# A decoder trunk with mixture of experts on one core: expert outputs weighted and added in place, the row list as one product, and reordered scores, taps and copies

## The reference, cut to what matters

```
y, _, v_rows = mixer(x)        # z = rms_norm(x) @ w_in -> u, v, a, b (512 channels each)
                               # v = layer_norm(gelu(v)); A = u * (masked 128x128 mix of v per chunk)
                               # B = silu(layer_norm(depthwise conv of a*sigmoid(b), width 31))
x = x + concat(A, B) @ w_out
x = x + attention(rms_norm(x) @ wq, K, V) @ wo     # prompt: K, V of 256 memory rows
                                                   # sample: 8 cached K, V sets, one for each token
g   = argmax(group logits)                         # 4 groups, 8 experts in each
w_e = softmax(top 2 logits of group g) * softmax(group logits)[g]
x = x + sum over the 2 experts of w_e * (silu(xt@w1) * (xt@w3)) @ w2      # inner width 256
y = rms_norm(x) * final_norm_g
```

## Time and profile before

| what | us |
|---|---|
| median of 3 runs | 679.25 (678.85 to 681.24) |
| the profiled execution's own time | 680.17 |
| its span in the trace | 678.4 |
| TensorE busy in it | 594.8 (88%) |
| VectorE busy | 317.4 (47%) |
| ScalarE busy | 197.9 (29%) |
| POOL busy | 79.8 (12%) |
| bytes moved | 181.57 MB, mean 268 GB/s |
| TensorE's mean granted clock | 0.944 |

### The profile page before, as it was taken

One profiled execution on the slowest core, in us unless ns is written; L12 is line 12 of the kernel. 1 busy time (PEld: TensorE's weight loads), 2 busy tenths in 40 slices (PEclk: granted clock), 3 DMA queues, 4 the chain that ended last, 5 costly groups with the idle time before them and its releaser, 6 DMA issues.

```text
span 678.4 us, 11951 instructions
## 1 busy us (share of the span) xinstructions
PE 594.8 (88%) x4899; PEld 466.9 (69%) x4899; DVE 317.4 (47%) x625; ACT 197.9 (29%) x337; POOL 79.8 (12%) x131
## 2 busy tenths in 40 slices
PE   5999999899999999999999957999999987589810
PEld 5999996577899999984889844546646654246400
DVE  4678787789644374778422273211111111011147
ACT  6422323145734344445022231111111111011032
POOL 0000000700002200000212201112112111010100
PEclk9999999999999999999989975999999999689965
DMA  8863110326554314779599495999999999999663
GB/s 325 306 243 124 63 64 3 127 84 212 164 167 149 125 64 137 271 243 424 208 391 393 160 399 199 402 421 418 420 417 420 421 418 421 420 421 414 250 271 127
DMA packets 35652, 181.57 MB, mean 268 GB/s; under 512 B 8943, under 2 KB 10127, under 8 KB 16765
## 3 DMA queue, kind: packets, MB, share of 16 engines
q1 hardware_dynamic: 26733, 165.62, 62.1%
q0 software_dynamic: 5600, 12.76, 5.0%
q10 hardware_dynamic: 3264, 2.42, 1.1%
HBM read 174.94 MB, written 15.61 MB: 281 GB/s over the span
## 4 chain that ended last, share of the span: by engine, by line
PE 65%; SPq 14%; DMA 8%; DVE 8%; issue 3%; ACT 1%; DVEq 0%; POOLq 0%; ACTq 0%
PE ps L1714 13%; PE ps L1716 13%; PE ps L1715 13%; SPq L628 9%; PE ps L2146 7%; SPq L637 4%; PE ps L2174 4%; DMA w<-exp_w 4%; PE ps L1821 4%; PE ps L1710 3%; DMA raw<-caches 2%; PE ps L1923 2%; DVE ttr_out L1354 1%; PE ps L1987 1%; DVE x L1662 1%
## 5 line engine op out<-in xcount | busy, mean ns | idle before, releaser
L1714 PE MATMUL ps<-xH,w_h 128*128 128x260 f32 x480 | 138.7, 289 | 0.4 <-DVE xL L1368 0.2
L1716 PE MATMUL ps<-xL,w_h 128*128 128x260 f32 x480 | 136.3, 284 | 0.0
L1715 PE MATMUL ps<-xH,w_l 128*128 128x260 f32 x480 | 136.1, 284 | 0.0
L2146 PE MATMUL ps<-w,xeT 128*64 128x256 f32 (+2 forms) x1024 | 121.5, 407 | 12.5 <-DMA w<-exp_w 10.3
L2146 PEld LDWEIGHTS ps<-w,xeT 128*64 128x64 f32 (+2 forms) x1024 | 82.9, 145 | 56.2 <-issue 29.5
L1714 PEld LDWEIGHTS ps<-xH,w_h 128*128 128x128 f32 x480 | 91.1, 190 | 5.0 <-issue 4.3
L1715 PEld LDWEIGHTS ps<-xH,w_l 128*128 128x128 f32 x480 | 91.1, 190 | 0.1
L1716 PEld LDWEIGHTS ps<-xL,w_h 128*128 128x128 f32 x480 | 91.1, 190 | 0.0
L1059 DVE TENSOR_TENSOR w_l<-raw,w_h 128x2048 fp32r<-128x2048 f32 x27 | 61.8, 2289 | 27.8 <-ACT w_h L741 27.6
L2174 PE MATMUL ps<-w,aT 128*64 128x512 f32 (+2 forms) x256 | 60.3, 628 | 15.8 <-DVE aT L1627 12.0
L741 ACT ACTIVATE w_h<-raw 128x2048 fp32r<-128x2048 f32 x27 | 51.6, 1911 | 22.2 <-PE ps L1716 19.3
(11 more groups left out here) (352 smaller groups left out, 857.0 us busy)
## 6 DMA issues: line engine op xcount, KB each, us to landing
w<-exp_w SPq DMA_DIRECT2D x96, 1024.0 KB, 24.0
raw<-weights SPq DMA_DIRECT2D x27, 1024.0 KB, 5.3
raw<-caches SPq DMA_DIRECT2D x16, 1024.0 KB, 7.4
qb<-q_rows POOLq DMA_DIRECT2D x4, 1024.0 KB, 6.7
yr<-y_rows SPq DMA_DIRECT2D x4, 1024.0 KB, 7.9
xT<-x_turned SPq DMA_DIRECT2D x4, 520.0 KB, 7.4
raw<-x_prompt SPq DMA_DIRECT2D x4, 512.0 KB, 12.0
x_rows<-x ACTq DMA_DIRECT2D x4, 512.0 KB
```

The lines of the kernel that those rows point to most:

```text
L1714: pe.matmul(out, h1, h2, start=start, stop=False)
L1715: pe.matmul(out, l1, h2, start=False, stop=False)
L1716: return pe.matmul(out, h1, l2, start=False, stop=stop)
L2146: last = pe.matmul((mm[0][half, j, 0:FF], ta[1][half, 0:FF])[h], xeT[j][:, k, half], w13[s][:, h, k, :], start=k == 0, stop=k == KT_D - 1)
```

## The change

Parts, in the order of the program:

1. V_TAPS is 11: VectorE does eight more part taps, TensorE 640 small products where it did 704.
2. VectorE does the v rows' scale and shift itself: two instructions for each piece and head, the first (x − mean) · gain, the second times the root plus bias. POOL does none of it.
3. VectorE's and ScalarE's order around the last sample scores is new. ScalarE: values_out(0), norms(3), split_h(25). VectorE: below.
4. The samples' outputs are turned by eight plain 128x128 transposes in two halves ("so0", "so1"), and copied from every 16th column.
5. The weights' five instructions stand ahead of count_p. A factor 0.5 doubles the weights, for part 7.
6. The list is one accumulation of ten products with `row_hot` as the stationary side and 32 moving columns; norm factor and weight are listed by ten more with 64 (`hot_two`). No parts.
7. VectorE adds the experts' output, times its slot's weight, onto the gathered rows (`rows_out`). Since both rows of a token now hold x + 2·w·y, their sum is twice the result; the final norm takes 4·EPS for that. The residual isn't read back, and the tail has one addition.
8. There are four row buffers `xe` in place of two and two `ye`. A gather into one waits for the scatter out of it. The third and fourth are cleared by POOL after the first two gathers.
9. The loop turns its first round's rows at its start; before, the last static round did that.
10. `kept_busy` adds products of ones with ones, whose result nobody reads: 14 at the start, 4 and 2 around the count, 20 ahead of the list, 12 and 4 around the first turn.
11. Some semaphores are merged, and ScalarE's table for Sqrt is loaded right after the loop.

```diff
-V_TAPS = 9
+V_TAPS = 11
+ROWS = 4
...
-            PART_AT = {4: 3, 5: 4, 6: 4, 7: 3, 8: 2, 9: 3, 10: 3, 11: 3, 14: 3}
+            PART_AT = {4: 3, 5: 4, 6: 4, 7: 3, 8: 2, 9: 3, 10: 3, 11: 3, 12: 2, 13: 2, 14: 3, 15: 2}
...
-                    last = dve.tensor_scalar(row, row, mv[0:n_t, j, h, 0:1], mv[0:n_t, j, h, 1:2], ALU.subtract, ALU.mult)
+                    last = dve.scalar_tensor_tensor(row, row, mv[0:n_t, j, h, 0:1], ln_g[0:n_t, c], ALU.subtract, ALU.mult)
                 last.then_inc(v_norm, 1)
+                dve.wait_ge(v_norm, j + 1)
+                for h in range(HEADS):
+                    row, n_t, c = v_row(j, h)
+                    last = dve.scalar_tensor_tensor(row, row, mv[0:n_t, j, h, 1:2], ln_b[0:n_t, c], ALU.mult, ALU.add)
+                last.then_inc(v_ready, 1)
...
-            sample_scores(5)
+            sample_scores(5, range(2))
             score_sums(3)
+            sample_scores(5, range(2, 4))
+            values_low(0)
+            sample_scores(6, range(2))
+            values_low(1)
             split_l(25)
-            values_low(0)
-            values_low(1)
-            sample_scores(6)
             values_low(2)
+            sample_scores(6, range(2, 4))
             values_low(3)
             sample_scores(7)
...
             dve.tensor_tensor(w_ex[:, 0, :], e_max[:, 1, :], e_max[:, 0, :], ALU.subtract).then_inc(g_dif, 1)
+            dve.wait_ge(g_exp, 1)
+            dve.tensor_reduce(g_sum[:], g_ex[:], AX_X, ALU.add)
+            dve.wait_ge(g_exp, 2)
+            link(dve.tensor_scalar(w_ex[:, 1, :], w_ex[:, 0, :], 1.0, 0.5, ALU.add, ALU.mult))
+            link(dve.tensor_tensor(w_ex[:, 1, :], w_ex[:, 1, :], g_sum[:], ALU.mult))
+            link(dve.reciprocal(wgt[:, 0, :], w_ex[:, 1, :]))
+            link(dve.tensor_tensor(wgt[:, 1, :], wgt[:, 0, :], w_ex[:, 0, :], ALU.mult))
...
+            dve.tensor_tensor(hot_two[:, :, :, 0, :], hot_col[:], rs_b, ALU.mult).then_inc(rs_hot_ready, 1)
+            dve.tensor_tensor(hot_two[:, :, :, 1, :].rearrange("p i t c -> p (i t) c"), hot_col[:].rearrange(flat),
+                              columns_of(wgt[:]), ALU.mult).then_inc(rs_hot_ready, 1)
...
-            def y_right(q, j, scattered):
+            def rows_out(q, i, weight):
...
-                dve.tensor_copy(ye[j][:, 512:D], mm[1][:, 1, :]).then_inc(yv_ready, 1)
+                for b in range(2):
+                    half = xe[i][:, 512 * b:512 * b + 512]
+                    dve.scalar_tensor_tensor(half, mm[1][:, b, :], weight, half, ALU.mult, ALU.add).then_inc(y_ready, 1)
...
-                link(dve.scalar_tensor_tensor(x2[0:n, t, :], yr[t][0:n, 0, :], wgt[0:n, 0, t:t + 1], x2[0:n, t, :],
-                                              ALU.mult, ALU.add))
-                dve.scalar_tensor_tensor(x2[0:n, t, :], yr[t][0:n, 1, :], wgt[0:n, 1, t:t + 1], x2[0:n, t, :],
-                                         ALU.mult, ALU.add).then_inc(y_sum, 1)
+                dve.tensor_tensor(x2[0:n, t, :], yr[t][0:n, 0, :], yr[t][0:n, 1, :], ALU.add).then_inc(y_sum, 1)
...
+            def kept_busy(out, count):
+
+                for _ in range(count):
+                    pe.matmul(out, ones[:], ones[:], start=True, stop=True)
+
+            pe.wait_ge(dve_made, 1)
+            kept_busy(ta[0][:, 0:P], 14)
             first_pair()
...
-            for k in range(8):
-                last = pe.matmul(out[:, k, :], o_s[:, k * P:(k + 1) * P], one_row, start=True, stop=True)
-            last.then_inc(tv_ready, 1)
+            for b in range(2):
+                pe.wait_ge(tv_used, TV_AT[f"or{b}"] + 1)
+                out = open_tv(f"so{b}")
+                for k in range(4):
+                    last = turn(out[:, k * P:(k + 1) * P], o_s[:, (4 * b + k) * P:(4 * b + k + 1) * P])
+                last.then_inc(tv_ready, 1)
...
+            pe.wait_ge(ta_used, len(TA_ORDER))
+            kept_busy(ta[1][:, 0:P], 20)
+            listed("ids", lambda n, i, j: hot_no[0:n, i, j, :])
+            pe.wait_ge(rs_hot_ready, 2)
+            listed("rs_ids", lambda n, i, j: hot_two[0:n, i, j].rearrange("p w c -> p (w c)"))
...
+            kept_busy(ta[1][:, 0:P], 12)
             pe.wait_ge(tv_used, len(TV_ORDER))
-            pe.wait_ge(ta_used, len(TA_ORDER))
-            gathered_columns(0, 0, 1)
+            gathered_columns(0, 1)
+            kept_busy(ta[1][:, 0:P], 4)
             for q in range(PAIRS):
                 hidden(q, q % 2, slots_of(q), q >= 2)
-                gathered_columns(q + 1, (q + 1) % 2, (q + 1) // 2 + 1)
+                if q + 1 < PAIRS:
+                    gathered_columns((q + 1) % ROWS, (q + 1) // ROWS + 1)
...
             for q in range(PAIRS):
                 pool.wait_ge(xt_done, q + 1)
-                gather(q % 2, gids[:, q + 2:q + 3])
-                pool.wait_ge(ya_ready, q + 1)
-                pool.wait_ge(yv_ready, q + 1)
-                scatter(q, q % 2, ids[:, q:q + 1])
+                i = (q + 2) % ROWS
+                if q + 2 >= ROWS:
+                    pool.wait_ge(y_stored[i], 16 * scattered(i, q + 2))
+                gather(i, gids[:, q + 2:q + 3])
+                pool.wait_ge(y_ready, 2 * (q + 1))
+                scatter(q % ROWS, ids[:, q:q + 1])
```

276 lines of the change are left out of this document (120 added, 156 removed).

## The result

The changed kernel takes 675.85 us in the median of 10 runs (673.57 to 677.55), the kernel before 679.37 (10 runs, 678.14 to 681.24): a ratio of 0.9947, with a 95% interval of 0.9932 to 0.9962. It is faster by 3.5 us where 7.95 was forecast. The profiled execution took 676.56 with a span of 674.8, so the two spans differ by 3.6.

The account below looks back on a forecast made before the run. TensorE was taken to hold most of the chain, then the expert-weight stream, restarted by round 0's gate. Terms sum to −7.95 from the profiled 680.17, giving 672.2; the median, 0.92 lower, was forecast at 671.4 us, range 665.5 to 678.

Parts of the forecast that it names:

- step (b): Routing: twenty products of ones ahead of the list take 6.0 us, ending just behind the one-hot rows it needs.
- step (d): Routing: twelve ones and second list end before the gather lands; turn takes 1.15 for 1.94, gate starts 418.7 for 417.55.
- Rival B's half-way case: Routing: the clock rises only in the list, so routing costs about +5 and the total is 676.5; chance 0.10.
- step (a): Routing: weight instructions ahead of count_p wait for the second exponential, putting count_p at 398.4, +2.0 us for the chain.
- Values: Values and sample scores: values_low(1) stands behind scores awaiting query rows, making TensorE late by +2.0 us, between 0 and 3.7.
- Sample rows: Turning the samples' outputs: eight transposes in halves start the output projection 1.4 earlier, clock staying up saves 1.6; −3.0 us.
- Rival C: Behind the sample rows: transposes leave the clock low, 1.6 us is lost, total 673.0; chance 0.08.
- Taps: Convolution: 64 of 704 products go, −2.4 us; v rows on VectorE cost nothing, with 3 us left at the take.
- Start: Program start: fourteen ones let the first pair run at full clock; −0.25 us, between 0 and −0.75.
- Loop entry: First loop round: its turn and copy move into the loop, 2.5 us at full clock, partly absorbed by weight waits; +1.1.
- Rival D: Rounds: gathers wait for scatters, which needs landings over 19 us; chance 0.07 together with Rival E.
- Rival E: Convolution stage: the v rows are late on VectorE by 11 us, total 682; chance 0.07 together with Rival D.

Follow-up runs that it names:

- e2: The changed kernel with VectorE's and ScalarE's order around the sample scores as before; 673.06 us, ratio 0.9905.
- e4: The changed kernel with V_TAPS back to 9, so 704 convolution products as before; 680.26 us, ratio 1.0003.
- e5: The changed kernel with the samples' outputs turned by products of 8 columns again, in the same two halves; 676.19 us, ratio 0.9946.
- e6: The changed kernel with the v rows' scale and shift on POOL again; 676.33 us, ratio 0.9961.
- e3: The changed kernel with the five weight instructions moved from ahead of count_p to behind row_hot; 671.65 us, ratio 0.9900.
- e11: The kernel before, unchanged, profiled a second time; 678.87 us in one execution.
- e1: The changed kernel without the 42 products of ones in routing, the 14 at the start kept; 676.74 us, ratio 0.9955.
- e12: e8 without the 14 products of ones at the start; 671.83 us, ratio 0.9892.
- e13: The kernel before with only 14 products of ones added ahead of the first pair; 677.27 us, ratio 0.9970.
- e10: The kernel before with the first of each tile's two additions in the tail left out, residual still read back; 673.38 us, ratio 0.9913.
- e7: The changed kernel with the changes of e2 and e3 together, all ones kept; 669.35 us, ratio 0.9850.
- e8: e7 without the twelve products of ones ahead of the first turn; 669.29 us, ratio 0.9843.
- e14: e8 with 7 products of ones at the start in place of 14; 669.26 us, ratio 0.9851.
- e9: e3 without the 42 products of ones in routing; 674.88 us, ratio 0.9936.

## Why the prediction was wrong

**Routing, step (b) and step (d): the steps that failed.** The prediction had "eight slow, twelve fast, 6.0 us" for the twenty ones, and the twelve ones ending before the gather. The first took 7.4, 14 or so at the lower level, for the clock rose only near 406, 6 us after they began and not 3.5. (In e2, e4, e5 and e6 it rose 2.8 to 5.4 us after they began and they took 5.9 to 7.1, so this part of the miss is between nothing and 1.4.) The lists took 2.6 and 2.9 us where 2.1 was taken. The twelve were half as fast as counted, because the clock falls under the second list or just as it ends (in all ten traces with ones ahead of the lists), and they held the turn for 2 us. 1.4 + 0.5 + 2.0 = 3.9 us is the miss of 3.95. The prediction had named a sign of being wrong, that ones are the bound in front of the list: they were, by 1.9 us. The estimate from one row at 417.55, where wide gate products raised the clock in 3.5 us, didn't carry over. Rival B's half-way case, with a chance of 0.10 and a price of about 676.5, comes nearest: it has the clock up only in the list, and it rose 1.4 us ahead of it.

**The weights' wait, step (a)**, was forecast as +2.0 and measured so (395.39 − 380.65 in place of 396.39 − 383.79: 2.1). What the forecast missed is what hangs on it. It named the small products queued behind count_p, and not that the clock, up at 1.00 ahead of TensorE's idle, falls in it or just behind it, so that the ones have a clock to raise and not one to keep (e3: 3 to 4 us for moving five small instructions).

**Values.** The mechanism was right, +2.0 was too small: 2.7 us of waiting and then half the clock for the value products, +3.4 in all, just under the upper end of 3.7. e2 shows it.

**Sample rows: the other step that failed.** −3.0 forecast, −2.27 measured, but that they are near is luck: the form is worth 0.8 (e5), the halves nothing, and the clock's part was one execution's (e11). Against the three other traces with the old form the gain is 0.6 us. Rival C doesn't apply: with transposes and with products the clock stayed up. The Trainium skill, "TensorE: Matmul & The Clock Gate", section "Part 4: PE-mode transpose", has it that transposes don't bring the full clock; in e1, e2, e12 and e13 the granted clock stayed at 1.00 through all of routing's 32 transposes, and in the twelve other traces, the changed kernel's among them, it fell to 0.50 and rose again while they ran. Neither is explained by the kind of product alone.

**Taps.** The taps gave 2.4, as forecast (2.6 between the convolution's ends of e4 and the changed kernel, 2.4 counted from the first turn). The v rows on VectorE took 2.3 us a tile as estimated and were hidden, with 0.45 us to spare at the take and not the forecast's 3. That the convolution gained 2.2 more was not foreseen: it is what the start's ones bring by themselves in e13 (49.7 to 47.5), 1.7 us of it the idle.

**Start.** The first pair indeed ran at the upper level (1.34 us for 2.07), and nothing came of it here, which is the lower end of what was argued; what the ones do bring, they bring in the convolution. The +0.28 lies inside what executions differ by there (85.6 to 86.8 among all kernels).

**Loop entry, `rows_out`, tail**: right, with their mechanisms (e10 for the tail). At the loop's entry the first gate products start 6.35 us behind the start of the last static round's `down` in place of 3.63 (620.99 − 614.64, 618.60 − 614.97), 2.7 us for the forecast's 2.5. The turn that left that static round gives 0.5 back, and waits that only the kernel before has further on take up 1.1. Rival D found no wait in the static rounds: the scatter landed in time. Rival E is out by the trace: the v rows end at 131.5, and VectorE then idles for 0.45 us before it takes the convolution's result.

**The sum.** The terms give 672.22 and, less 0.92, 671.3; the prediction has 671.4.

The best versions here are e7, e8 and e14, all at 669.3 us: 1.5% faster than before and 1% faster than the changed kernel, for two parts of the change taken back.

## What to carry to other kernels

Filler products are products whose result nobody reads. Here they brought nothing measurable with an idle of 2 us ahead of them, and some 2.5 us without it, when their end lay under another engine's work; even then the clock fell in one trace of five. So look first for the wait in front of them: one misplaced wait of 2 us cost more than the fillers could return. Work that waits for a slow transfer must not stand in an in-order queue ahead of work that another engine waits for, however short it is. Take a clock's fall or rise from more than one execution before you put it in a sum.

## What the runs showed of the hardware

- An idle of 1.7 us on TensorE that no semaphore released ("issue") stood at one place of the convolution in all three traces of kernels with before's start (before, e10, e11), 0.9 us in e12, and in none of the twelve with 7 or 14 products of ones at the start (the changed kernel, e1 to e9, e13, e14). What e13 adds is 28 records at 1.1 us, and the idle at 127 is gone. In e10 the clock fell behind the idle (0.50 in 130:132) and the convolution ended 1.5 us later still. The number of instructions ahead of the place may matter; e14 has seven fewer than the changed kernel and no idle, and nothing but products at the start was tried. The cause stays open.
- A product of ones of 128x128 takes 0.42 us at 1.2 GHz and 0.24 at 2.4 GHz (40 records, two for each product, in 4.73 us in e3), not half. The first figure is from the start of the changed kernel, 28 records in 5.92 us. The windows print 1.00 there, but they hold as many records as windows at 0.50: eleven in 2:4 and eleven in 402:404. At the start of an execution the pace of the products says more than the printed clock.
- The same stretch of transposes had the clock at 1.00 in e1 and at 0.50 for about 3 us in the changed kernel and the kernel before. A term that rests on the clock in such a stretch is uncertain by 1 to 2 us, an estimate from these 3 us at half speed.
- The clock can fall while TensorE is never idle: it went from 1.00 to 0.50 under the second list's ten products with 64 moving columns, or just as they ended, in all ten traces with ones ahead of the lists (402.4 in e7, 412.6 in the changed kernel), and under products of ones in e12.
- VectorE's subtractions of 128x128 took 0.28 us each until POOL began and 0.78 each beside POOL's products and sums in e6 (four in 1.11 us from 120.46, twelve in 9.36 from 121.56). With POOL idle the changed kernel's two-input instructions of that size took 0.29 each (four in 1.14).
